# Evicting first in two attentions, with the relative bias as an identity product on TensorE

## What is computed

```python
logits = einsum("bqhc,bqkc->bhqk", qb, c_sel) * scale
dist = q_pos[None, :, None] - sel
logits = logits + rel_bias[t5_bucket(dist)]        # a bias per head and distance
p = softmax(where(dist >= 0, logits, -inf))
out = einsum("bhqk,bqkc->bqhc", p, c_sel)
```

## Time and profile before

| what | value |
|---|---|
| median of 3 runs | 3579.27 us (3573.62 to 3580.11) |
| the profiled execution, its own time | 3577.13 us |
| its span in the profile | 3575.2 us |
| TensorE busy (matmuls) | 3283.7 us, 92% of the span |
| VectorE busy | 1841.7 us, 52% |
| ScalarE busy | 971.4 us, 27% |
| GpSimd busy | 901.1 us, 25% |
| mean granted TensorE clock | 0.943 of 2.4 GHz |
| first attention | from about 660 to 1097 us |
| second attention | from about 3080 to 3442 us |

### The profile page before, as it was taken

One profiled execution on the slowest core, in us unless ns is written; L12 is line 12 of the kernel. 1 busy time (PEld: TensorE's weight loads), 2 busy tenths in 40 slices (PEclk: granted clock), 3 DMA queues, 4 the chain that ended last, 5 costly groups with the idle time before them and its releaser, 6 DMA issues.

```text
span 3575.2 us, 36793 instructions
## 1 busy us (share of the span) xinstructions
PE 3283.7 (92%) x14026; PEld 2485.9 (70%) x14026; DVE 1841.7 (52%) x3008; ACT 971.4 (27%) x1810; POOL 901.1 (25%) x566
## 2 busy tenths in 40 slices
PE   7999999878779998989999999998997998899898
PEld 4577788555557886668887788887866886555467
DVE  1599991566664447871331544443334326756551
ACT  2420111355552003560001100001214114654340
POOL 0132332000002324653332433332233352100002
PEclk9899999898989999999999999999998999998679
DMA  8012332100001110112332111112112110000012
GB/s 207 12 48 66 91 103 93 60 18 8 17 18 42 48 41 34 44 48 95 102 133 89 36 52 49 47 48 100 61 53 78 48 47 15 1 1 12 0 50 81
DMA packets 185861, 196.37 MB, mean 55 GB/s; under 512 B 12257, under 2 KB 152029, under 8 KB 184029
## 3 DMA queue, kind: packets, MB, share of 16 engines
q1 hardware_dynamic: 170669, 142.08, 13.6%
q10 hardware_dynamic: 15024, 51.98, 3.9%
HBM read 153.15 MB, written 40.89 MB: 54 GB/s over the span
## 4 chain that ended last, share of the span: by engine, by line
PE 69%; DVE 9%; issue 9%; ACT 4%; POOL 4%; DMA 2%; DVEq 2%; POOLq 1%; ACTq 1%; SPq 0%
PE psum L625 66%; PE psum L629 3%; DVE arena L1681 3%; DVE arena L1684 2%; DVE rounded L1681 1%; ACT arena L1292 1%; POOL stat L1166 1%; POOL arena L1220 1%; DVE arena L1832 1%; DMA arena<-z_d 1%; POOL rounded L1177 1%; ACT arena L1402 1%; POOL arena L1237 1%; DVE arena L2207 1%; ACTq L1298 0%
## 5 line engine op out<-in xcount | busy, mean ns | idle before, releaser
L625 PE MATMUL psum<-rounded,rounded 128*128 128x512 f32 (+2 forms) x9504 | 2200.6, 392 | 85.1 <-DVE rounded L1681 44.8
L625 PEld LDWEIGHTS psum<-rounded,rounded 128*128 128x128 f32 x9504 | 1799.7, 191 | 458.0 <-issue 89.0
L625 PE MATMUL psum<-arena 128*128 128x512 f32 (+15 forms) x2450 | 778.9, 494 | 38.3 <-ACT arena L1292 15.5
L1175 POOL CAST rounded<-arena 128x1024 fp32r<-128x1024 f32 (+1 forms) x190 | 205.9, 1084 | 1738.2 <-DMA arena<-in_w_in 826.3
L625 PEld LDWEIGHTS psum<-arena 128*128 128x128 f32 (+4 forms) x2450 | 408.2, 205 | 334.2 <-issue 269.1
L1292 ACT ACTIVATE arena<-psum 128x512 f32<-128x512 f32 (+9 forms) x572 | 307.2, 566 | 754.4 <-PE psum L625 707.3
L1177 POOL TENSOR_TENSOR rounded<-arena,rounded 128x1024 fp32r<-128x1024 f32 (+1 forms) x190 | 466.6, 2456 | 28.2 <-issue 1.3
L629 PE MATMUL psum<-ident,arena 128*128 128x128 f32 (+1 forms) x1816 | 303.6, 313 | 150.4 <-ACT arena L1292 48.7
L629 PEld LDWEIGHTS psum<-ident,arena 128*128 128x128 f32 (+1 forms) x1816 | 242.6, 159 | 239.9 <-issue 92.0
L1681 DVE TENSOR_TENSOR arena<-arena,psum 128x512 f32<-128x512 f32 (+1 forms) x176 | 125.8, 733 | 355.2 <-PE psum L625 335.4
L1681 DVE TENSOR_TENSOR rounded<-arena,rounded 128x1024 fp32r<-128x1024 f32 (+1 forms) x132 | 198.2, 1532 | 210.8 <-ACT rounded L1295 210.2
(11 more groups left out here) (137 smaller groups left out, 1505.0 us busy)
## 6 DMA issues: line engine op xcount, KB each, us to landing
arena<-in_w_in SPq DMA_DIRECT2D x84, 512.0 KB, 3.8
arena<-in_w_ffn_up SPq DMA_DIRECT2D x44, 512.0 KB, 3.8
arena<-in_w_ffn_down SPq DMA_DIRECT2D x22, 512.0 KB, 3.6
z_d<-arena ACTq DMA_DIRECT2D x32, 256.0 KB, 3.0
gate_d<-arena ACTq DMA_DIRECT2D x16, 512.0 KB, 3.9
arena<-in_w_ssm_out SPq DMA_DIRECT2D x16, 512.0 KB, 4.0
arena<-z_d SPq DMA_DIRECT2D x8, 1024.0 KB, 4.8
arena<-gate_d ACTq DMA_DIRECT2D x16, 512.0 KB, 3.3
```

What stands on the lines that cost most here:

```text
L625: return pe.matmul(out, lhsT, rhs, start=start, stop=stop)
L1175: pool.tensor_copy(high_part, raw)
```

## The change

In both attentions, ScalarE and VectorE first do what older units wait for and then turn to the newest one. In the first attention the bias no longer is subtracted in PSUM by VectorE: TensorE adds it to the score tile between the high and the low product, as a float32 product of the identity with the bias tile, whose sign is turned once at the start.

```diff
@@ TensorE, first attention @@
+            pe.wait_ge(bias_in, 16)
             for s in range(STEPS1):
...
                     for lo, hi in chunks(u["nk"] * P):
                         k_high, k_low = u["k"](lo, hi)
                         mm(out[:, lo:hi], u["q"], k_high, True, False)
+                        w = u["nk"] * P
+                        near = max(lo, w - 256)
+                        if near < hi:
+                            mm(out[:, near:hi], ident[:, :], biasT[:, u["h"], near - w + 256:hi - w + 256], False, False)
                         last = mm(out[:, lo:hi], u["q"], k_low, False, True)
@@ ScalarE, first attention @@
             for s in range(STEPS1):
-                if s in stacked_at1:
-                    stack_highs(stacked_at1[s])
-                if s < N1:
-                    u = units1[s]
-                    act.wait_ge(*written(("S", s)))
...
+                if s - 1 in summed_at1:
...
+                    copy(attT[half, h // 2, here], name, psum_of(name)[half, :])
...
                 if s in turned_at1:
...
-                if s - 1 in summed_at1:
...
+                if s < N1:
+                    u = units1[s]
+                    act.wait_ge(*written(("S", s)))
+                    p = probs1[s % len(probs1)][:, 0:u["nk"] * P]
+                    act.activation(p, p, ACT.Exp, scale=-1.0, bias=negmax[:, s % 4:s % 4 + 1],
+                                   accum_out=rsum[:, s % 8:s % 8 + 1]).then_inc(exp_ready, 1)
+                if s in stacked_at1:
+                    stack_highs(stacked_at1[s])
                 if s in split_at1:
@@ ScalarE, second attention @@
             for s in range(STEPS2):
+                if s in turned_at:
...
                 if s < len(subs2):
...
-                if s in turned_at:
...
@@ VectorE, start @@
-            dve.tensor_copy(bias_row[0:HEADS, :], psum_of("bias")[0:HEADS, 0:384]).then_inc(empty("bias"), 1)
+            dve.tensor_scalar(bias_row[0:HEADS, :], psum_of("bias")[0:HEADS, 0:384], -1.0, None, ALU.mult).then_inc(empty("bias"), 1)
@@ VectorE, first attention @@
-            dve.wait_ge(bias_in, 16)
 
             for s in range(STEPS1):
-                if s - 1 in stacked_at1:
-                    stack_lows(stacked_at1[s - 1])
-                if s < N1:
...
-                    tt_(out[:, lo:w], out[:, lo:w], biasT[:, u["h"], 256 - (w - lo):256], ALU.subtract)
-                    dve.drain()
...
                 n = s - 2
                 if 0 <= n < N1:
...
                     dve.tensor_scalar(p, p, r, None, ALU.mult).then_inc(probs_ready, 1)
+                if s < N1:
...
+                    dve.tensor_tensor_reduce(
...
+                if s - 1 in stacked_at1:
+                    stack_lows(stacked_at1[s - 1])
@@ VectorE, second attention @@
             for s in range(STEPS2):
-                if s < len(subs2):
...
                 n = s - 2
...
                 if s - 1 in summed_at:
...
                         tt_(z, o, z, ALU.mult).then_inc(empty(name), 1)
+                if s < len(subs2):
...
```

More of the change, by code:

```diff
@@ L1633, in _ @@
             for s in range(STEPS2):
+                if s in turned_at:
+                    n = turned_at[s]
+                    u = subs2[n]
+                    pT = pT2[u["i"] // 4]
+                    if (u["i"] % 4 == 0 or u["ph"] == "e") and sweep_before(n) is not None:
+                        act.wait_ge(*completed(sweep_before(n)))
+                    here = slice((u["i"] % 4) * P, (u["i"] % 4 + 1) * P)
+                    for grp in range(last_group(u) + 1):
+                        name = ("T", N1 + n, grp)
+                        if u["ph"] == "e":
+                            copy(pT[:, grp, :], name)
+                            continue
+                        m = min(4, u["nk"] - 4 * grp)
+                        copy(pT[:, 4 * grp:4 * grp + m, here], name,
+                             psum_of(name)[:, 0:m * P].rearrange("p (a b) -> p a b", b=P))
                 if s < len(subs2):
@@ L2246, in _ @@
                         tt_(z, o, z, ALU.mult).then_inc(empty(name), 1)
+                if s < len(subs2):
+                    u, name = subs2[s], ("S", N1 + s)
+                    w = u["nk"] * P
+                    dve.wait_ge(*completed(name))
+                    held = held_by(s)
+                    if u["ph"] == "e":
+                        dve.tensor_reduce(negmax4[u["four"]], psum_of(name).rearrange("p (a b) -> p a b", b=MEMT),
+                                          axis=AX.X, op=ALU.min).then_inc(maximum4, 1)
+                    else:
+                        if held is not None and not first_map(subs2[held]):
+                            dve.wait_ge(*completed(("T", N1 + held, last_group(subs2[held]))))
+                        dve.tensor_tensor_reduce(
+                            out=probs2[probs_slot(s)][:, 0:w], in0=psum_of(name)[:, 0:w], in1=u["mask"], scale=1.0, scalar=3e38,
+                            op0=ALU.add, op1=ALU.min, accum_out=negmax[:, s % 4:s % 4 + 1]).then_inc(empty(name), 1)
                 for j in range(2):
```

65 lines of the change are left out of this document (16 added, 49 removed).

## The result

The changed kernel takes **3518.76 us** in the median of 4 runs (3508.64 to 3524.39), the kernel before 3576.44 in the median of its 4. The ratio is 0.9835 with a 95% interval of 0.9809 to 0.9861: 58 us faster, where 21 were foreseen and the range ended at 3530. The profiled execution took 3524.39 us (span 3522.4) at a mean granted clock of 0.956, against 3577.13 (3575.2) at 0.943.

The account below looks back on a forecast made before the run. It took the first attention as bound by PSUM bank turnaround on top of TensorE's work, the second's idle time as mostly behind VectorE. First attention -4, second -17: -21 us on 3577.13 gives 3556.1, median 3558 us; range 3530 to 3592.

Parts of the forecast that it names:

- The identity product, 51 us of TensorE's work with its loads hidden: First attention: bias products add 3.2 us per head, 51 us over 16 heads, to TensorE; identity weight loads cost nothing.
- The new stall of 3.0 us on the key banks: First attention, each head: a score tile waits 3.0 us for banks freed late by the key stack at step 2's end.
- ScalarE's order removes the three stalls: First attention: copies before exponentials remove TensorE's waits of 2.30, 2.33 and 0.87 us in a head.
- This is worth nothing by itself: First attention: taking the bias subtraction, some 52 us in all, off VectorE gains nothing, as TensorE does not wait for VectorE.
- A head at the full clock, 24.8 us: First attention: period of a head at full clock after the change, 24.8 us, the same as before.
- The clock, +1.7 us in every head: First attention: the new stall mostly brings one slow-clock stretch per head, costing 1.7 us, so 26.5 us a head.
- The rival that it stays up: First attention: the clock stays up with one stall per head in place of three; 3536 us, chance 0.20.
- -5 was the term: First attention: 13 heads at -0.37 us each give -5 us; first and last two heads together +1.
- MLA, 7 of 8.0 us: Second attention, MLA: VectorE's new order removes 7 of TensorE's 8.0 us of waits before transposes for the z product.
- Differential branch, -10: Second attention: 8 of 9.2 us of waits for value-product copies and half of 4.0 for the square go.
- In the memory branch TensorE has no idle time, so no gain: Second attention, memory branch: the change gains nothing, since TensorE has no idle time there.
- ScalarE's new order is covered by the same lack of waits: Second attention: ScalarE's new order costs nothing, as none of TensorE's longer waits is for ScalarE's copies.

Follow-up runs that it names:

- run 8: Run 4's kernel with every identity product issued twice, so the bias is added twice: 3516.25 us, ratio 0.9855.
- run 4: Changed kernel with the stacking of the next head's keys back at the start of its step on ScalarE and VectorE (early stack): 3478.16 us, ratio 0.9745.
- 15: Changed kernel with only ScalarE's high part of the key stack back at the step's start, VectorE's low part still last: 3477.00 us, ratio 0.9733.
- run 11: Run 4's kernel with ScalarE's old order in the first attention (exponential first, value product's copy last): 3530.30 us, ratio 0.9881.
- run 10: Run 4's kernel with VectorE's old order in the first attention (maximum first, then scaling): 3476.32 us, ratio 0.9729.
- run 2: Kernel before with both engines' new orders in the first attention only, the bias still subtracted on VectorE: 3554.93 us, ratio 0.9959.
- run 12: Changed kernel, late key stack kept, without the identity product, so with no bias: 3490.70 us, ratio 0.9766.
- run 7: Run 4's kernel with the bias subtracted by VectorE in place of the identity product: 3494.19 us, ratio 0.979.
- run 9: Run 4's kernel without any bias, neither product nor subtraction: 3458.71 us, ratio 0.9679.
- run 3: Kernel before with the identity product in place of VectorE's subtraction, all orders as before: 3558.60 us, ratio 0.9971.
- run 5: Kernel before with only VectorE's new order in the second attention, ScalarE's kept old: 3541.57 us, ratio 0.9931.
- run 13: Kernel before with both engines' new orders in the second attention only from step 128, where the memory units begin: 3570.30 us, ratio 0.9997.
- run 14: Kernel before with both engines' new orders in the second attention only before step 128 (MLA and differential branch): 3529.74 us, ratio 0.9883.
- run 1: Kernel before with both engines' new orders in the second attention alone: 3534.52 us against 3571.41, ratio 0.9899.

## Why the prediction was wrong in size

Right in direction and in several steps, but less than half of the size: the parts gave -58.7 us where the sum had -21. The step that failed most is the reading of the second attention by TensorE's idle time alone. TensorE's busy time there was itself stretched by a low clock, and that was worth some 10 us in the differential branch and all of the 9.3 in the memory branch, which the sum put at nothing. In the first attention the terms for a head at the full clock and for the clock were too large by 12 us together, and the stretches outside the 13 heads lacked 6.

- **The identity product, 51 us of TensorE's work with its loads hidden: right.** Run 8 measured 49.9 for a second one, and the score tiles beside it 0.43 us for the first too.
- **The new stall of 3.0 us on the key banks: right**, 2.76 to 3.4 us, 14 times and not 15, from the chain that was named; runs 4 and 15 took it away and with it 40 us.
- **ScalarE's order removes the three stalls: right**, and with the early stack and the product it is the whole of the orders' gain in the first attention (run 11: 51.5 us; VectorE's, run 10: nothing).
- **"This is worth nothing by itself", of the subtraction that leaves VectorE: wrong.** This step failed by its argument: TensorE didn't wait for VectorE by name, but what released ScalarE's exponential, and behind it the copies, was the maximum behind the subtraction. With the stack late it is worth 31.5 us (run 2 against run 12), with the stack early 37.0 (run 7 against run 9). In the kernel before, the swap alone gains 13 us (run 3), though the product brings 50 us of work. The failed step hardly shows in the sum, and that is luck. The step on ScalarE's order had taken off all waits of the old kind and expected none behind VectorE, which the orders alone don't bring about: with the subtraction kept, 28.7 us of waits behind the maximum appear (run 2). The changed kernel has 2.6 us of them. Kept or swapped, the two kernels with the late stack are nearly even (429.1 and 426.4 us).
- **A head at the full clock, 24.8 us: too long.** It took 24.01, 24.02, 24.69 and 24.71, 24.36 in the mean; -0.4 for 13 heads is 6 us. The stall was 2.76 to 2.91 us there in place of 3.0; where the rest comes from was not tried.
- **The clock, +1.7 us in every head: mis-sized.** It fell behind 10 of the 14 stalls and not behind the other 4, and cost 25.57 - 24.36 = 1.2 us a head. The rival that it stays up came true for a third of the heads. The step rested on one stall of 2.72 us; the trace of before also has one of 2.73 us, at 723.49, that was followed by the full clock:

```profile
723.49:727.09 3.60, 2.58 (x16) 2.01 (x16) 3.19 (x11) 2.02 (x5) 0.00 (x0) 1.00 0.00 0
```

Together the 13 heads gave -16.8 us, where -5 was the term; before the first and behind the last of them it was another -5.3, where +1 was.
- **MLA, 7 of 8.0 us: nearly right** (-8.8). Run 5 shows that VectorE's order alone gives 3.2 of it: the two orders share it, where the prediction gave it to VectorE.
- **Differential branch, -10: half.** TensorE's idle time fell by 8.4 us (16.8 to 8.4), as foreseen. The other 10 us are the same work at a clock of 0.77 in place of 0.70, which the step left out though the earlier trace rows had the 0.68.
- **"In the memory branch TensorE has no idle time, so no gain": wrong**, -9.3 us. The busy time was itself stretched by a clock of 0.74; 60.5 us of busy became 47.4, and what did it lies ahead of the branch (runs 13 and 14). Its 5.9 us of idle time are one wait before the output product, so a clock of 0.74 with no wait inside the branch was there to be read before.
- **"ScalarE's new order is covered by the same lack of waits": wrong** by 8 us of the second attention (run 1 against run 5), once VectorE's copies no longer came last.

By parts, the forecast was short by 18 us in the first attention and by 20 in the second. The profiled execution of the changed kernel was the slowest of its four; its median is 6 us below.

## What to carry to other kernels

Read a stretch that is full but slow as carefully as one with idle time: if TensorE is busy at half of its clock, the gain may lie in what comes ahead of it, and a removed wait is worth its length plus what the clock gives back. An instruction on an engine that "nobody waits for" is on the path if the engine that is waited for waits for it; moving 50 us of work onto the busiest engine gained 13 us with the old orders and 16 with the early stack (3 in the changed kernel as it stands), because it filled waits, shortened the chain behind them and went with a higher clock. And when an order is turned to "old work first", look for the one thing that is not old work: the key stack has to stay early, which was worth 40 us, nearly twice what the whole change gained in the first attention (22 us).

## What the hardware showed that was not expected

- Equal stalls, unequal clock. In the changed kernel the same wait for the key banks, in two heads, was followed by these 3.6 us (windows, the clock behind the brackets):

```profile
797.56:801.16 3.60, 3.60 (x20) 2.89 (x21) 3.41 (x8) 1.57 (x6) 0.00 (x0) 1.00 0.02 5
872.62:876.22 3.60, 3.60 (x13) 3.22 (x14) 2.81 (x7) 1.16 (x4) 0.00 (x0) 0.50 0.00 0
```

The stalls were 2.76 and 2.91 us. Stalls of either length stand on both sides in other heads, and near the end of this attention one of only 1.94 us, at 1065.39, was followed by 0.63. So length alone doesn't tell. With no bias at all (run 12) the stalls were 3.18 to 3.77 us from 692 to 1004 us, and the clock fell behind each of the 14. In run 4, with none over 2.1 us from the first score tile on, it fell behind none of those of 0.9 us or more. What tips a stall in between was not settled.
- The lower level can hold while TensorE is drawn as busy without a gap: 30 us in run 13, with 64-row score products and transposes as the work, and the same work ran at 2.4 GHz in run 14 (67.7 us of memory branch against 55.3).
- The drawn starts hide what a product costs. The two instructions of an identity product of 256 columns show 0.24 us from their start to the next start (793.10 to 793.34), and yet a score tile is 0.43 us longer for each such product (run 8). Its weight loads add nothing to that.
